# A hybrid layer stack on one core: query sums, table use and gate chain reordered in the local attention, and the end of a depthwise convolution rearranged

## The reference

```
sq = rms_norm(sq.reshape(B, L, SWA_HEADS, SWA_HD), q_norm)      # 8 heads of 64
sk = rms_norm(sk.reshape(B, L, SWA_KV_HEADS, SWA_HD), k_norm)
s = einsum(q, k) / sqrt(hd) - slopes * dist ; masked to a window of 128
m = max(max(s), sink); p = exp(s - m)
p = p / (sum(p) + exp(sink - m)); o = p @ v
log_a = log_sigmoid(glr @ w_alpha2 + b_alpha) / 16              # the gate chain
b = cumsum(log_a) within chunks of 64; qe = q * exp(b); ke = k * exp(-b)
...
u = a * sigmoid(gate)
u = depthwise_conv(u, w_dw) + b_dw                              # 31 taps, causal
u = silu(layer_norm(u, ln_g, ln_b)) @ w_pw2 + b_pw2
```

## Time and profile before

| | us |
|---|---|
| median of 3 runs | 1744.71 (1744.37, 1744.71, 1747.96) |
| the profiled execution, its own time | 1743.44 |
| its span, first to last instruction | 1741.5 |
| TensorE busy | 1711.8 |
| VectorE / ScalarE / GpSimd busy | 942.6 / 608.1 / 185.2 |
| granted TensorE clock, mean | 0.997 |

### The profile page before, as it was taken

One profiled execution on the slowest core, in us unless ns is written; L12 is line 12 of the kernel. 1 busy time (PEld: TensorE's weight loads), 2 busy tenths in 40 slices (PEclk: granted clock), 3 DMA queues, 4 the chain that ended last, 5 costly groups with the idle time before them and its releaser, 6 DMA issues.

```text
span 1741.5 us, 21892 instructions
## 1 busy us (share of the span) xinstructions
PE 1711.8 (98%) x8088; PEld 1367.2 (79%) x8088; DVE 942.6 (54%) x1264; ACT 608.1 (35%) x894; POOL 185.2 (11%) x158
## 2 busy tenths in 40 slices
PE   9989999999999999999999999999999999999998
PEld 7768888888888866477888888888777788888886
DVE  5675546652665389857532343365873754234432
ACT  4553434431444232254321222243453432122221
POOL 0210211100111101110200011100000021001111
PEclk9999999999999999999999999999999999999999
DMA  6111223332223245311332323212211233322221
GB/s 231 62 53 56 85 82 97 96 121 88 93 87 107 84 136 158 100 63 59 121 97 97 93 92 97 94 60 86 72 37 34 74 109 98 97 86 96 97 83 48
DMA packets 48883, 157.84 MB, mean 91 GB/s; under 512 B 7088, under 2 KB 7728, under 8 KB 48816
## 3 DMA queue, kind: packets, MB, share of 16 engines
q1 hardware_dynamic: 48288, 155.45, 27.8%
q10 hardware_dynamic: 528, 1.46, 0.3%
HBM read 146.14 MB, written 2.10 MB: 85 GB/s over the span
## 4 chain that ended last, share of the span: by engine, by line
PE 90%; DVE 5%; ACT 2%; issue 1%; SPq 1%; DMA 0%; POOL 0%; DVEq 0%; ACTq 0%; POOLq 0%
PE bank L1133 26%; PE bank L1134 26%; PE bank L1135 26%; PE bank L1284 1%; PE bank L1669 1%; PE bank L1290 1%; PE bank L1285 1%; DVE cv L2281 1%; PE bank L1223 1%; DVE w_lo L1910 1%; SPq L484 1%; DVE swa_p L2013 1%; PE bank L1177 1%; PE bank L1839 1%; ACT w_hi L676 0%
## 5 line engine op out<-in xcount | busy, mean ns | idle before, releaser
L1910 DVE TENSOR_TENSOR w_lo<-w_raw,w_hi 128x1024 fp32r<-128x1024 f32 x269 | 347.3, 1292 | 313.0 <-ACT w_hi L676 190.1
L1133 PE MATMUL bank<-a_hi,w_hi 128*128 128x512 f32 x1156 | 460.6, 398 | 0.1
L1134 PE MATMUL bank<-a_lo,w_hi 128*128 128x512 f32 x1156 | 456.5, 395 | 0.0
L1135 PE MATMUL bank<-a_hi,w_lo 128*128 128x512 f32 x1156 | 454.3, 393 | 0.0
L1134 PE MATMUL bank<-g_lo,w_hi 128*128 128x512 f32 x688 | 272.0, 395 | 0.0
L1133 PE MATMUL bank<-g_hi,w_hi 128*128 128x512 f32 x688 | 270.8, 394 | 0.0
L1135 PE MATMUL bank<-g_hi,w_lo 128*128 128x512 f32 x688 | 269.0, 391 | 0.0
L1133 PEld LDWEIGHTS bank<-a_hi,w_hi 128*128 128x128 f32 x1156 | 218.1, 189 | 55.9 <-issue 6.0
L1135 PEld LDWEIGHTS bank<-a_hi,w_lo 128*128 128x128 f32 x1156 | 218.1, 189 | 48.5
L1134 PEld LDWEIGHTS bank<-a_lo,w_hi 128*128 128x128 f32 x1156 | 218.5, 189 | 46.4 <-issue 1.0
L676 ACT ACTIVATE w_hi<-w_raw 128x1024 fp32r<-128x1024 f32 x153 | 159.8, 1050 | 163.8 <-PE bank L1135 150.7
(11 more groups left out here) (290 smaller groups left out, 1807.6 us busy)
## 6 DMA issues: line engine op xcount, KB each, us to landing
w_raw<-in_stream SPq DMA_DIRECT2D x269, 512.0 KB, 3.5
shifted<-u_pad SPq DMA_DIRECT2D x120, 66.0 KB, 2.0
h<-in_xT SPq DMA_DIRECT2D x8, 256.0 KB, 5.5
out<-h SPq DMA_DIRECT2D x8, 256.0 KB, 2.1
cst_b<-in_consts SPq DMA_DIRECT2D x1, 896.0 KB, 9.7
cst_b<-in_consts ACTq DMA_DIRECT2D x1, 896.0 KB, 6.3
shifted<-u_pad ACTq DMA_DIRECT2D x8, 66.0 KB, 2.4
tap_cols<-in_vectors SPq DMA_DIRECT2D x16, 29.2 KB, 1.8
```

Source lines behind the costliest of these rows:

```text
L1133: pe.matmul(out, w0, x0, start=start, stop=False, skip_group_check=loose)
L1134: pe.matmul(out, w0, x1, start=False, stop=False, skip_group_check=loose)
L1135: return pe.matmul(out, w1, x0, start=False, stop=stop, skip_group_check=loose)
L1910: dve.tensor_tensor(w_lo[slot][:, :], w_raw[slot][:, :], f(w_hi[slot][:, :]), ALU.subtract)\
```

## The change

In the local attention: the order of the units is changed so that the query tiles come at fillers 8 and 9 and the low-rank tile at 10. The sums of query tiles 3 and 4 go to bank 3, one of the score banks, both in pair 0 behind `swa_values(0)`; one root takes both in pair 1, and the scores of pair 2 wait for it in place of the transposes. The logits and with them the whole gate chain come one pair later (logits in pair 1; Identity, Abs, Exp and Ln in pair 2; gate and first scan behind pair 2, the second scan ahead of pair 3's scores, the copy of the chunk ends behind pair 3). The two small operations of a head's maximum become one, with the negated sinks prepared once. ScalarE's weight copies stand between the two heads of a pair and at its end, and VectorE's weight splits after the copies of transposes. Below, ACT's and VectorE's loops are shown as they are after the change.

In the convolution: the last tile has 24 taps on TensorE and six on VectorE. All buffers for shifted rows get 532 instead of 528 columns, those for tap matrices 768 instead of 640. GpSimd also adds tile 6. The product of the mean with GpSimd's sum comes ahead of the last group of four taps of the last tile, in bank 0, and one product with tile 7 finishes the mean. VectorE adds TensorE's sum of tile 5 ahead of building the last matrices and that of tile 6 right behind. The last fold of squares is left to TensorE as a further `ln_sum`.

```diff
+TAPS_LAST = 24
+COPIES_SP = 8
+TAP_COLS = TAPS_LAST * GROUP
-Z_UNITS = [15, 16, 17, 18, 4, 0, 1, 5, 10, 2, 3, 6, 7, 8, 9, 11, 12, 13, 14]
+Z_UNITS = [15, 16, 17, 18, 4, 0, 1, 5, 2, 3, 10, 6, 7, 8, 9, 11, 12, 13, 14]
-        RW = SEQ + TAPS_STACKED - SHIFTS
+        RW = SEQ + TAPS_LAST - SHIFTS
...
@@ ScalarE, local attention (after) @@
             for j in range(SWA_H // 2):
                 n2 = z0 + 8 + 2 * j
                 if j:
                     swa_pt_of(2 * j - 1)
                 swa_exp_of(2 * j)
                 if j == 0:
                     act.wait_ge(sv_turned, 1)
                     act.activation(z_vs[:, :], bank[7][:, :], ACT.Copy).then_inc(sv_copied, 1)
                 if j == 1:
                     swa_square(4, T(z_sq, 3), 10)
                 if j == 2:
                     gla_logit_of(0)
                     gla_logit_of(1)
                 w_hi_of(n2 + AHEAD, (n2 + AHEAD) % RING)
                 swa_exp_of(2 * j + 1)
                 if j == 0:
                     swa_square(3, T(z_sq, 2), 9)
                 if j == 1:
                     swa_root(3, 2)
                 if j == 2:
                     act.wait_ge(gla_y, 2)
                     act.activation(gla_e, gla_b, ACT.Abs).then_inc(a_chain, 1)
                 if j:
                     swa_out_of(j - 1)
                 swa_pt_of(2 * j)
                 if j == 2:
                     act.wait_ge(a_chain, 1)
                     act.activation(gla_e, gla_e, ACT.Exp, scale=-1.0).then_inc(a_chain, 1)
                     act.wait_ge(a_chain, 2)
                     act.activation(gla_e, gla_e, ACT.Ln, bias=1.0).then_inc(gla_l, 1)
                 if j == 3:
                     act.wait_ge(gla_cum, 2)
                     act.activation(gla_e, gla_b, ACT.Exp, scale=1.0 / 16).then_inc(gla_exp, 1)
                 w_hi_of(n2 + 1 + AHEAD, (n2 + 1 + AHEAD) % RING)
             swa_pt_of(SWA_H - 1)
...
@@ TensorE, local attention @@
-                token_sums(bank[4][:, 8 * n:8 * n + 8], swa_sq_buf(n), halves).then_inc(swa_sums, 1)
+                token_sums(bank[4 if n < 3 else 3][:, 8 * n:8 * n + 8], swa_sq_buf(n), halves).then_inc(swa_sums, 1)
...
+                if t == 2:
+                    pe.wait_ge(swa_rms, 4)
...
-                if i % 2 == 0 and i <= 4:
-                    pe.wait_ge(swa_rms, 3 + i // 2)
+                if i == 0:
+                    pe.wait_ge(swa_rms, 3)
+                if i == 4:
+                    pe.wait_ge(gla_y, 2)
...
-                if j == 0:
+                if j == 1:
                     gla_logits()
                 if j + 1 < SWA_H // 2:
                     filler(n + 1, 0)
                     swa_values(j)
-                    if j < 2:
-                        if j == 0:
-                            pe.wait_ge(gla_y, 2)
-                        swa_sums_of(3 + j)
+                    if j == 0:
+                        pe.wait_ge(swa_bias, 3 * NB)
+                        swa_sums_of(3)
+                        swa_sums_of(4)
                     filler(n + 1, 1)
...
@@ VectorE, local attention (a head's maximum; then the loop after) @@
-                dve.tensor_scalar(nm, nm, SWA_HD ** -0.5, col("sinks", swa_head(i)), ALU.mult, ALU.max)\
+                dve.tensor_scalar(nm, nm, -SWA_HD ** -0.5, no_sinks[:, swa_head(i):swa_head(i) + 1], ALU.mult, ALU.min)\
                     .then_inc(swa_mx, 1)
-                dve.wait_ge(swa_mx, 2 * i + 1)
-                dve.tensor_scalar(nm, nm, -1.0, None, ALU.mult).then_inc(swa_mx, 1)
...
             lo_ahead(8)
             lo_ahead(9)
             for j in range(1, SWA_H // 2):
                 n = 7 + 2 * j
                 swa_pt_of(2 * j - 1)
                 if j == 3:
                     gla_cumulate(1)
                 swa_softmax_in(2 * j)
                 filler_out(n)
                 swa_softmax_in(2 * j + 1)
                 swa_normalise(2 * j)
                 lo_ahead(n + 1)
                 swa_normalise(2 * j + 1)
                 swa_out_lo(j - 1)
                 if j == 1:
                     swa_r_of(3, 2)
                 filler_out(n + 1)
                 swa_pt_of(2 * j)
                 lo_ahead(n + 2)
                 if j == 2:
                     gla_log_gate()
                     gla_cumulate(0)
                 if j == 3:
                     dve.wait_ge(gla_cum, 2)
                     dve.tensor_copy(b_last[:, :], chunks[:, :, CHUNK - 1]).then_inc(gla_blast, 1)
                     dve.wait_ge(gla_exp, 1)
                     dve.scalar_tensor_tensor(z_q[:, :], z_q[:, :], GLA_DK ** -0.5, gla_e, ALU.mult, ALU.mult)\
                         .then_inc(gla_ops, 1)
...
@@ GpSimd @@
             add_tile(KD - 4)
             add_tile(KD - 3)
+            add_tile(KD - 2)
...
@@ TensorE, convolution @@
-                for t in range(TAPS_STACKED // SHIFTS):
+                for t in range(stacked(k) // SHIFTS):
+                    if t == stacked(KD - 1) // SHIFTS - 1:
+                        pe.wait_ge(out_read, TILE0["pw2"])
+                        pe.wait_ge(mean_add, KD - 1)
+                        pe.matmul(bank[0][:, :], cst[:, MEAN:MEAN + P], ssum[:, :], start=True, stop=False)
...
-            pe.wait_ge(out_read, TILE0["pw2"])
-            run_idle(0, 2)
-            pe.wait_ge(mean_add, KD - 2)
-            pe.matmul(bank[4][:, :], cst[:, MEAN:MEAN + P], ssum[:, :], start=True, stop=False)
-            for k in (KD - 2, KD - 1):
-                pe.wait_ge(cv_ready, k + 1)
-                last = pe.matmul(bank[4][:, :], cst[:, MEAN:MEAN + P], T(cv, k), start=False, stop=(k == KD - 1))
-            last.then_inc(mean_done, 1)
-            run_idle(0, 2)
-            run_idle(0, 2)
+            run_idle(6, 1)
+            pe.wait_ge(cv_ready, KD)
+            pe.matmul(bank[0][:, :], cst[:, MEAN:MEAN + P], T(cv, KD - 1), start=False, stop=True).then_inc(mean_done, 1)
+            run_idle(6, 2)
+            run_idle(6, 2)
...
             ln_sum(2, False, False)
-            run_idle(0, 1)
+            run_idle(6, 1, 192)
             pe.wait_ge(ln_folded, 1)
-            ln_sum(4, False, True).then_inc(stat_done, 1)
+            ln_sum(4, False, False)
+            pe.wait_ge(ln_folded, 2)
+            ln_sum(6, False, True).then_inc(stat_done, 1)
...
@@ VectorE, convolution @@
+            add_pe_taps(KD - 3)
             build_taps(KD - 1)
-            tap_ops(KD - 1, 0, taps_dve)
-            add_pe_taps(KD - 3)
             add_pe_taps(KD - 2)
+            tap_ops(KD - 1, 0, taps_dve(KD - 1))
             add_pe_taps(KD - 1)
             lo_ahead(UNIT0["pw2"])
...
-            for k, other in ((4, 5), (6, 7), (4, 6)):
-                ...
+            for k in (4, 6):
+                dve.wait_ge(sq_ready, SQ0["ln_var"] + k + 2)
+                dve.tensor_tensor(T(m, k), T(m, k), T(m, k + 1), ALU.add).then_inc(ln_folded, 1)
```

More of the change, by code:

```diff
@@ L201, in program @@
         decay = sb("decay", [P, 2 * NCH])
+        no_sinks = small[:, 0:SWA_H]
         sq_buf = [tmp[4][:, 0:SEQ], tmp[5][:, 0:SEQ]]
@@ L475, in program, with stacked, shifted_copies @@
         mla_parts = ((5, 0, SEQ), (6, SEQ, 2 * SEQ), (7, 2 * SEQ, N_PROB))
-        def shifted_copies(queue, k, turns):
+        def stacked(k):
+            return TAPS_LAST if k == KD - 1 else TAPS_STACKED
+        def shifted_copies(queue, k, first=0, last=SHIFTS * P // GROUP, landed=None):
             if k >= 3:
                 queue.wait_ge(tap_sums, k - 2)
-            for a in turns:
-                for g in range(P // GROUP):
-                    sh = (g + a) % SHIFTS
-                    queue.dma_start(shifted[k % 3][sh * GROUP:(sh + 1) * GROUP, g * RW:(g + 1) * RW],
-                                    u_pad[k % 4][g * GROUP:(g + 1) * GROUP, sh:sh + RW])\
-                        .then_inc(shifted_landed[k % 3], 16)
+            for c in range(first, last):
+                a, g = divmod(c, P // GROUP)
+                sh = (g + a) % SHIFTS
+                queue.dma_start(shifted[k % 3][sh * GROUP:(sh + 1) * GROUP, g * RW:(g + 1) * RW],
+                                u_pad[k % 4][g * GROUP:(g + 1) * GROUP, sh:sh + RW])\
+                    .then_inc(landed or shifted_landed[k % 3], 16)
         def conv_bank(c):
@@ L544, in _ @@
                     sp.wait_ge(u_ready, k + 1)
-                    shifted_copies(sp, k, range(SHIFTS if k < KD - 1 else SHIFTS // 2))
+                    if k < KD - 1:
+                        shifted_copies(sp, k)
+                    else:
+                        shifted_copies(sp, k, 0, COPIES_SP)
             uq_first, uq_last = UNIT0["uq"] // RING - 1, (UNIT0["uq"] + 5) // RING - 1
@@ L753, in swa_root @@
                 c = RC_SWA + 8 * n
-                act.activation(rms[:, c:c + 8 * count], bank[4][:, 8 * n:8 * (n + count)], ACT.Sqrt,
+                act.activation(rms[:, c:c + 8 * count], bank[4 if n < 3 else 3][:, 8 * n:8 * (n + count)], ACT.Sqrt,
```

(35 more changed lines are left out.)

102 lines of the change are left out of this document (35 added, 67 removed).

## The result

The changed kernel takes 1725.26 us (median of four runs, 1723.97 to 1726.86), the kernel before 1744.54 (four runs, 1742.32 to 1747.96): ratio 0.9888 with a 95% interval of 0.987 to 0.9907, 19.3 us less. The forecast was 13 less, 1731.7, and its range ended at 1727.5.

The account below looks back on a forecast made before the run. TensorE's instruction stream plus about 30 us of pauses was taken to bound the kernel. Local attention 6.85 and convolution with norm 5.5 sum to 12.35 us off, giving 1731.7 us, range 1727.5 to 1737.5.

Parts of the forecast that it names:

- the reference of the sum: Whole kernel: 12.35 us taken off the profiled execution's 1743.44 gives 1731.1; by the runs' median 1732.4.
- Attention, 6.85 forecast: Local attention: 5.25 us from head 7's transposes starting earlier plus 1.6 from full clock behind them.
- head 6 at 122.41: Local attention: TensorE starts head 6 at 122.41, not 125.40, after a pause of 2.4 us behind the gate chain.
- the clock's fall: Local attention: the 2.4 us pause ahead of head 6 lowers the clock, so head 7 starts at 127.6, not 125.98.
- rival 1: Local attention: the clock holds after the 2.4 us pause, 0.9 us less, about 1730.8; chance 0.66 together with the forecast.
- Rival 2: Gate chain: Ln finds its table loaded, pause ahead of head 6 shrinks to 1.1 us; gain 14.5, 1729.4; chance 0.08.
- Rival 3: Gate chain longer than worked out, 3 us more delaying heads 6 and 7; gain 3.5 + 5.5, 1734.5; chance 0.10.
- Convolution, 5.06 forecast: Convolution's end: VectorE subtracts the mean from 726.26, before 731.32; the last taps' start left at 718.00.
- Norm, 0.45 forecast: Behind the mean: without the last fold, the sum over squares ends 0.45 us earlier.
- the price of the mean's pause: Convolution's end: removed idle products, pause, and three products at low clock, 4.37 us against 2.67 at full clock.
- Rivals 4 and 5: Convolution gives some 2 of 5.5 us, 1735, chance 0.10; wider rows slow the shifted copies, 1750, chance 0.03.
- the middle reference (1744.05): Whole kernel: forecast 1731.7 taken as the middle between 1731.1 by the profiled execution and 1732.4 by the runs' median.

Follow-up runs that it names:

- `silu_early`: Kernel before with one single-column Silu put ahead of need, so ScalarE's Silu table loads earlier: 1736.99 us, ratio 1.0.
- `ln_idle`: Changed kernel with the idle product behind `ln_sum(2)` widened from 192 to 512 columns: 1725.08 us, ratio 0.9932 against the kernel before.
- `attn_only`: Kernel before with only the local attention part of the change: 1729.72 us, ratio 0.9955.

## Why the prediction was right or wrong

**The step that failed** is the reference of the sum, "against the profiled execution's own 1743.44: 1731.1", with the median of the runs beside it: the forecast takes off 12.35 us and leaves all else as it stood in these executions, products at full clock included. That execution holds 6.8 us in which TensorE does the same products more slowly, in none of the pauses that the sum counted. The stretch is in none of the lines that the change touches, both kernels have it in single executions, and the profiled execution of the changed kernel in the first comparison doesn't hold it. In place of 1743.44 the kernel before has medians of 1737.0 to 1738.0 in four later comparisons, and by these the sum (12.35) gives about 1725.0, where the changed kernel stands (1724.55 to 1727.72). The trace of before had it to be read: the prediction speaks of "the distance of 0.2285 us that the products have elsewhere", and from 249 to 607 us of the same trace it is 0.2333. The timed runs of that first comparison were as slow, 1742.32 to 1747.96; they have no profile, so whether all held the stretch, and why all of them did, is open. The nearness of 1725.0 is in part luck: the attention gave more than forecast and the convolution less, as follows.

**Attention, 6.85 forecast, 6.52 measured in the first pair.** Each step: head 2 at 84.92 forecast, 85.15 measured; head 4 at 103.20, 103.43; head 6 at 122.41 behind a pause of 2.4, 122.74 behind 2.59; the clock's fall; head 7 at 127.6, 127.94. The 0.2 is there from head 2 on. In the four later profiles of the unedited changed kernel the clock holds behind the pause, which is still 2.6: values at 136.1 to 136.3, a gain of 7.4 against before's 143.6. That is rival 1 (7.75). The same pause is followed by either level, so that it "is nearest to the 2.33" was no ground to choose by. Two sums of this part don't come out as written: 84.92 goes with the logits at their whole 1.88 us, not at the 1.3 that the text gives them (that would be 85.5), and 132.82 less 127.6 is 5.22, not 5.25. The work between the first transposes and head 2's fell from 19.34 to 18.34 us, so the larger value was near.

**Rival 2 is refuted**: Ln has its own load of 1.28 at 105.95, and the next Exp one at 109.75. By the Trainium skill (ScalarE: Activation LUTs, "Table sets: the hidden batching unit"), one set holds both functions and a single load serves them; the trace of the changed kernel disagrees, with these two loads of 1.28 us, as that of before did. Rival 3 (a longer gate chain) didn't come: the scores began at 114.40, forecast 114.15.

**Convolution, 5.06 forecast, 4.78 measured.** The order came as worked out; tile 7 is added 6.62 us behind the last taps' start and not 6.42, since TensorE's four more taps end later, and the subtraction starts at 8.52 and not at 8.26. VectorE's six taps took 5.99 beside both of GpSimd's additions, and TensorE covered them. The last taps' start, which the forecast left where it was, is set by the last shifted copy, as shown above.

**Norm, 0.45 forecast, 1.30 lost.** The extra idle time is gone, but the clock falls there now. The second step that failed is the price of the mean's pause: 5.06 holds 1.7 us (4.37 less 2.67, three products at the low clock) as won for good. In the changed kernel's five profiles the low level came in the norm instead, and the old order doesn't always pay for it either (`silu_early`). With the clock held in both, the mean's gain is 3.4 us, which is 5.06 less that 1.7: the pause and the idle products were priced rightly, the clock wasn't. Mean and norm together take 24.91 us on average in five profiles of before and 21.23 in five of the changed kernel: 3.7 us are gained, where 5.5 were forecast. Where the clock held, in `ln_idle`, they take 20.14. The 0.45 itself isn't tested by that run, as its filler is 0.5 us longer. That the fall follows from what TensorE did before I haven't shown, and the filler that went with it didn't keep it away a second time. With 7.2 for the attention (143.60 to 136.38 on average) that makes 10.9, within the 9.3 to 13.1 that the medians give.

**Rivals 4 and 5.** The convolution did give less, 3.7, but by the clock in the norm, not by a pause of the mean. The wider rows cost nothing: from the first sums of squares to the last taps it is 110.75 before and 110.78 after (110.4 and 110.7 on average of five profiles each), and the copies of the first tile are issued in 11.47 us before and 11.39 after, so a copy isn't longer by anything that matters. By the middle reference (1744.05) the gains of rivals 2 and 3 give 1729.6 and 1735.1, not the 1729.4 and 1734.5 of the text; nothing hangs on it.

## What to carry to other kernels

Before summing against one execution, compare the distance of the same instructions in several far stretches of its trace, and against a second execution: a stream that is 2% slower at the full clock and without a pause shows in no table of waits, and here it was worth half as much as the change. Price a clock fall as a chance and not as won: here the low level stood in one of two neighbouring stages in 16 of 18 profiles, with the pause ahead of the mean and without it, so its price belongs into the range. When a wait is moved off a queue, the gain is the smaller of how far the moved step and the one behind it can go.

## What the runs showed of the hardware

- TensorE's products have two distances at the full granted clock, 0.2289 and 0.2333 us from start to start (1072 and 1052 products in 245 us). The larger one lasted for 257 to 358 us of the feed-forward in five of 18 profiles and ended there at the sums of one column, in each of them; for 6 to 54 us it comes in others too (179 to 233 in `attn_only`). The same program has the long stretch in one execution and not in the next.
- The granted clock fell to its 1.2 GHz level in sums of one column with TensorE busy throughout (0.58 in the stretch of 720 us). Behind the same pause of 2.6 us ahead of head 6 it fell in the first profile of the changed kernel and held in the four later ones. Ahead of the mean it fell behind pauses of 2.3 to 2.6 us in four of five profiles of before, and held behind 2.22 in the fifth and behind 2.61 in `silu_early`.
- With a wait for several things, the profile named VectorE's build at L2332, which had ended 0.6 us before the taps started; the last of the shifted copies had landed 0.09 us before.
